# Gathering the rows of a further job when those of the one before it are turned, and one condition per expert on GpSimd

## The reference, cut to what matters

```python
def hier_moe(h, w_rg, b_rg, w_re, b_re, w_gate, w_up, w_down):
    n, t_len, d = h.shape
    x = h.reshape(-1, d)
    ...                      # top-1 of 4 groups, then top-2 of its 8 experts: 2 experts of 32 per token
    hg = jnp.einsum('md,edf->mef', x, w_gate)
    hu = jnp.einsum('md,edf->mef', x, w_up)
    act = jax.nn.silu(hg) * hu * combine[..., None].astype(x.dtype)
    y = jnp.einsum('mef,efd->md', act, w_down)
    return y.reshape(n, t_len, d)
```

## Time and profile before

| | |
|---|---|
| time, median of 3 | 1289.67 us |
| the profiled execution's own time | 1288.67 us |
| its span (first to last instruction) | 1286.9 us |
| TensorE matmul busy | 1086.6 us (84%) |
| VectorE / ScalarE / GpSimd busy | 381.4 / 228.4 / 187.9 us |
| mean granted TensorE clock | 0.926 |
| DMA, mean | 219 GB/s |

### The profile page before, as it was taken

The page is one execution under the profiler, slowest core; times in us unless marked ns, Lnnn a source line. Parts: engine busy times, 40 slices in busy tenths (PEclk is TensorE's granted clock), DMA queues, the critical chain, the costliest instruction groups (busy, mean ns, idle before and its releaser), DMA issues.

```text
span 1286.9 us, 19486 instructions
## 1 busy us (share of the span) xinstructions
PE 1086.6 (84%) x7107; PEld 682.5 (53%) x7108; DVE 381.4 (30%) x731; ACT 228.4 (18%) x413; POOL 187.9 (15%) x297
## 2 busy tenths in 40 slices
PE   5999998899679978888499999999599866797790
PEld 4887685675345534444177777644355433353440
DVE  2000013342342111111239899352432101021116
ACT  4000111344201111011230100261101000110112
POOL 0000100100022221211102111010032212122120
PEclk9999998999889998888799999999799888898895
DMA  9323124700547999999741100421749998399545
GB/s 364 152 92 144 36 78 73 289 2 21 212 167 307 406 409 408 408 405 409 307 167 67 66 2 2 152 114 40 303 169 409 404 354 340 113 396 361 226 164 226
DMA packets 71938, 281.90 MB, mean 219 GB/s; under 512 B 11614, under 2 KB 11678, under 8 KB 68576
## 3 DMA queue, kind: packets, MB, share of 16 engines
q1 hardware_dynamic: 55824, 251.66, 50.3%
q0 software_dynamic: 10800, 17.89, 4.0%
q10 hardware_dynamic: 5216, 11.10, 2.6%
HBM read 269.83 MB, written 29.65 MB: 233 GB/s over the span
## 4 chain that ended last, share of the span: by engine, by line
PE 49%; DMA 26%; DVE 12%; issue 5%; ACT 4%; POOLq 1%; POOL 1%; ACTq 0%; SPq 0%; DVEq 0%
DMA ring<-w_moe 14%; PE psum L1496 10%; DMA ar<-w_moe 7%; PE psum L1685 5%; PE psum L1604 5%; PE psum L1816 5%; DVE ar L1353 4%; PE psum L1490 3%; PE psum L1779 3%; DMA ar<-normed_rows,ixe 3%; PE psum L1740 3%; PE psum L1713 2%; PE psum L1547 2%; PE psum L1563 1%; DVE ar L1142 1%
## 5 line engine op out<-in xcount | busy, mean ns | idle before, releaser
L1685 PE MATMUL psum<-ring,ar 128*64 128x256 f32 x1408 | 179.2, 400 | 21.2 <-DMA ring<-w_moe 19.4
L1685 PEld LDWEIGHTS psum<-ring,ar 128*64 128x64 f32 x1408 | 102.4, 144 | 95.3 <-issue 32.0
L1496 PE MATMUL psum<-ar,ring 128*128 128x272 f32 x576 | 132.7, 393 | 0.0
L1816 PE MATMUL psum<-ar,ring 128*128 128x272 f32 x512 | 120.8, 398 | 3.0 <-DVE ar L1339 3.0
L1496 PEld LDWEIGHTS psum<-ar,ring 128*128 128x128 f32 x576 | 109.3, 190 | 22.9 <-issue 0.3
L1816 PEld LDWEIGHTS psum<-ar,ring 128*128 128x128 f32 x512 | 97.8, 192 | 28.0 <-issue 4.2
L1353 DVE SCALAR_TENSOR_TENSOR ar<-ar,sv 128x512 f32<-128x512 f32 x120 | 107.0, 893 | 5.8 <-ACT ar L900 1.9
L1685 PE MATMUL psum<-ar 128*64 128x256 f32 x640 | 85.6, 414 | 14.9 <-DMA ar<-w_moe 14.9
L1282 DVE COPY ar<-psum 128x128 f32<-128x128 f32 x64 | 18.7, 292 | 265.8 <-PE psum L1730 265.8
L1740 PE MATMUL psum<-ring,ar 128*64 128x512 f32 x352 | 84.1, 598 | 0.8 <-DVE ar L1282 0.4
L1604 PE MATMUL psum<-ring,ar 128*128 128x512 f32 x192 | 84.0, 594 | 0.0
(11 more groups left out here) (216 smaller groups left out, 1162.6 us busy)
## 6 DMA issues: line engine op xcount, KB each, us to landing
ring<-w_moe SPq DMA_DIRECT2D x44, 3072.0 KB, 16.8
ar<-w_moe SPq DMA_DIRECT2D x20, 3072.0 KB, 16.8
ring<-w_mix SPq DMA_DIRECT2D x4, 3072.0 KB, 20.9
ring<-w_pw SPq DMA_DIRECT2D x6, 2048.0 KB, 10.7
ring<-expert_outputs SPq DMA_DIRECT2D x8, 1024.0 KB, 7.9
ring<-kv_in SPq DMA_DIRECT2D x2, 2880.0 KB, 11.6
normed_rows<-ar ACTq DMA_DIRECT2D x8, 512.0 KB, 2.6
X<-x_in ACTq DMA_DIRECT2D x4, 512.0 KB, 9.6
```

Of the source, the lines that this page charges most:

```text
L1496: t = mm(psum[:, b + h, 0:HALF], w[:, k, P * c:P * c + P], hT[:, k, HALF * h:HALF * h + HALF], start=k == 0, stop=k == KD - 1)
L1685: t = mm(psum[64 * f:64 * f + 64, u % 2, 0:2 * P], xt[:, k, 64 * (u % 2):64 * (u % 2) + 64], w[:, k, f, :], start=k == 0, stop=k == KD - 1)
L1816: t = mm(psum[:, b + h, 0:HALF], w[:, k, o:o + P], hT2[:, k, HALF * h:HALF * h + HALF], start=k == 0, stop=k == KD - 1)
```

## The change

On GpSimd `further_first` and `further_rest` become one function, `further(it, u)`, which reads the count and, only if it isn't zero, the number in front. For each chunk c of the expert it first issues the gather of the rows of chunk c + 1 of the whole list, whatever expert that belongs to, once chunk c has been turned, and then sends out the result of c. The gather of the list's first chunk is issued ahead of the loop without a condition. After the list's last chunk one more gather is issued, whose indices are all out of bounds (`SKIP`), so that it moves no rows; the index table `tg` gets one more column for it, which VectorE fills with one more instruction, and GpSimd now waits for four tables and not three. The other engines' code for the further jobs is unchanged.

```diff
--- before.py
+++ after.py
@@ -158,7 +158,7 @@
         ixg = sb("ixg", [P, 3], I32)
         ixe = sb("ixe", [P, 1], I32)
         ixy = sb("ixy", [P, 4], I32)
-        tg = mb[:, 0:4 * MORE].bitcast(I32)
+        tg = mb[:, 0:4 * MORE + 2].bitcast(I32)
         jt = sb("jt", [1, 2 * EXPERTS], I32)
         psum = ctx.enter_context(nc.psum_tensor("psum", [P, 8, 512], F32))
 
@@ -556,7 +556,7 @@
                 nc.gpsimd.memset(xg[0], 0.0).then_inc(moe.rows_clear, 1)
                 pool.wait_ge(moe.jobs, n + 1)
                 nc.gpsimd.memset(xg[1], 0.0).then_inc(moe.rows_clear, 1)
-                pool.wait_ge(moe.tokens, 3 * n + 3)
+                pool.wait_ge(moe.tokens, 4 * n + 4)
                 nc.gpsimd.memset(xg[2], 0.0).then_inc(moe.rows_clear, 1)
                 pool.wait_ge(moe.xn_out, 16 * TILES * (n + 1))
 
@@ -573,15 +573,12 @@
                     pool.indirect_dma_start(xg[v], None, xn_dram, bass.IndirectOffsetOnAxis(ixg[:, v:v + 1], 0),
                                             bounds_check=TOK - 1, oob_is_err=False).then_inc(moe.rows_in[v], 16)
 
-                def counts(it, u):
-                    return (pool.value_load(jt[0:1, bass.ds(MSLOTS * it + (EXPERTS * what + u), 1)],
-                                            min_val=0, max_val=MORE) for what in range(2))
 
                 def chunk_rows(chunk):
 
                     pool.wait_ge(ex[n].turned, chunk + 1)
-                    o = nc.s_assert_within(chunk + MORE, MORE, 2 * MORE - 1,
-                                           skip_runtime_bounds_check_because="at most MORE chunks")
+                    o = nc.s_assert_within(chunk + MORE, MORE, 2 * MORE,
+                                           skip_runtime_bounds_check_because="at most MORE chunks and one empty")
                     nc.gpsimd.tensor_copy(ixe[0:JOB, 0:1], tg[0:JOB, bass.ds(o, 1)]).then_inc(ex[n].ix, 1)
                     pool.wait_ge(ex[n].ix, chunk + 1)
                     pool.sem_inc(moe.seen, 1)
@@ -599,21 +596,18 @@
                     pool.indirect_dma_start(ys_dram, bass.IndirectOffsetOnAxis(ixy[:, 3:4], 0), ye, None,
                                             bounds_check=4 * TOK - 1, oob_is_err=False).then_inc(ex[n].out, 16)
 
-                def further_first(it, u):
-
-                    chunks, before = counts(it, u)
+                def further(it, u):
+
+                    def count(what):
+                        return pool.value_load(jt[0:1, bass.ds(MSLOTS * it + (EXPERTS * what + u), 1)],
+                                               min_val=0, max_val=MORE)
+
+                    chunks = count(0)
                     with pool.If(chunks > 0):
-                        chunk_rows(before)
-
-                def further_rest(it, u):
-
-                    chunks, before = counts(it, u)
-                    with pool.If(chunks > 0):
-                        with pool.If(chunks > 1):
-                            with pool.Fori(1, chunks) as c:
-                                chunk_rows(before + c)
-                                chunk_out(before + c - 1)
-                        chunk_out(before + chunks - 1)
+                        before = count(1)
+                        with pool.Fori(0, chunks) as c:
+                            chunk_rows(before + c + 1)
+                            chunk_out(before + c)
 
                 def outputs(it, u):
 
@@ -625,13 +619,11 @@
                     pool.indirect_dma_start(ys_dram, bass.IndirectOffsetOnAxis(ixy[:, b:b + 1], 0), yj[b], None,
                                             bounds_check=4 * TOK - 1, oob_is_err=False).then_inc(moe.y_out[b], 16)
 
-                def body(it, gathers, jobs=MSLOTS, last=False):
+                def body(it, gathers, jobs=MSLOTS):
                     for u in range(jobs):
                         if u % 2 == 0 and gathers:
                             rows_of(3 * it + (u // 2 + 4), u + 8)
-                        further_rest(it, u)
-                        if not (last and u == jobs - 1):
-                            further_first(it, u + 1)
+                        further(it, u)
                         outputs(it, u)
 
 
@@ -639,12 +631,16 @@
                     rows_of(v, 2 * v, True)
                 nc.gpsimd.memset(xe, 0.0).then_inc(pool_link, 1)
                 pool.wait_ge(pool_link, 3 + 2 * n)
-                further_first(0, 0)
+                nc.gpsimd.tensor_copy(ixe[0:JOB, 0:1], tg[0:JOB, MORE:MORE + 1]).then_inc(ex[n].ix, 1)
+                pool.wait_ge(ex[n].turned, 1)
+                pool.wait_ge(ex[n].ix, 1)
+                pool.indirect_dma_start(xe, None, xn_dram, bass.IndirectOffsetOnAxis(ixe[0:JOB, 0:1], 0),
+                                        bounds_check=TOK - 1, oob_is_err=False).then_inc(ex[n].rows, 16)
                 rows_of(3, 6)
                 with pool.Fori(0, 4) as it:
                     body(it, True)
                 body(4, False)
-                body(5, False, EXPERTS % MSLOTS, True)
+                body(5, False, EXPERTS % MSLOTS)
 
             experts(0)
 
@@ -1253,6 +1249,8 @@
                                             ALU.arith_shift_right).then_inc(moe.tokens, 1)
                 nc.vector.tensor_scalar(tg[0:JOB, MORE:2 * MORE], tb[0:JOB, EXPERTS:JOBS], 2, None,
                                         ALU.arith_shift_right).then_inc(moe.tokens, 1)
+                nc.vector.tensor_scalar(tg[0:JOB, 2 * MORE:2 * MORE + 1], psum[0:JOB, 7, 0:1], 0.0, float(SKIP),
+                                        ALU.mult, ALU.add).then_inc(moe.tokens, 1)
 
                 def keep_rows(pair, first=False):
```

## The result

The changed kernel takes 1253.99 us (median of 4 runs, 1252.19 to 1255.05) against 1289.76 us before: 35.8 us less, a ratio of 0.9723 with the 95% interval 0.9706 to 0.9739. The forecast was 1246.7 us, 43.0 less. The profiled execution has a span of 1252.5 us, 34.4 less than before. Two single executions further down lie far outside their rows of the table, one of 2246 us (last row) and one of 1474 us (reordered, again); they are counted in the medians and left out of the ratios.

The account below looks back on a forecast made before the run. The first expert stage was taken as bound by weights, the second as held up by further jobs' gathers. 35.6 + 10.0 - 1.0 - 1.0 - 0.2 - 0.4 = 43.0 us gained, giving 1246.7 us; range 1242 to 1258.

Parts of the forecast that it names:

- signs of being wrong: Second stage of 274 us or more, chunk windows above 10 us without a wait, or waits ahead of 15 and 23.
- The waits that go: TensorE's five waits for gathered rows ahead of second-stage chunks all vanish: 35.6 us gained.
- The clock: Five chunks slowed by reduced TensorE clock after waits would take 8.81 us each at full clock: 10.0 us gained.
- the clock stays down: Rival: the chunks' own 0.4 to 0.9 us pauses keep TensorE's clock low; 34.0 us gained, 1255.7 us; chance 0.08.
- What is late next: Three new delays: expert 11's second chunk 1.0 us, the weights 1.0 us, GpSimd's loop 0.2 us.
- Second chunk of 11: Its gather, issued after the first chunk's turning, would land late and make TensorE wait: 1.0 us lost.
- Weights late in the stage: The second stage's weight stream may fall behind TensorE near expert 31: 1.0 us lost, bounds 0 and 18.
- GpSimd's loop: GpSimd's 10.5 us of standing still would make expert 15's gather late: 0.2 us lost.
- The added work: One more VectorE instruction in each layer's setup delays clearing of `xg[2]`: 0.4 us lost in two layers.
- The removed work: 91 GpSimd table reads go in the second stage, 26 us of its sequencer's time; counted as no gain.
- The slower rival: GpSimd pauses with each looped expert would decide the pace; 1300 us at 5.55 us per pause; chance 0.02.

Follow-up runs that it names:

- last row: Kernel before, gathers in their old places, second table read only where an expert has chunks, plus 40 never-executed instructions per expert on GpSimd: 1302.44 us, ratio 1.0089.
- reordered, again: Second measurement of the changed kernel with chunks moved ahead of pair turning (TensorE), product (VectorE) and pair gather (GpSimd): 1243.81 us, ratio 0.9626.
- the pauses filled: Changed kernel with useless matmuls in TensorE's pauses inside and ahead of chunks: 1253.28 us, ratio 0.9712.
- the reordered kernel: Changed kernel with chunks moved ahead of the next pair's turning on TensorE, the product on VectorE and the pair's gather on GpSimd: 1244.46 us, ratio 0.9642.
- the changed kernel's second: Changed kernel measured again, unaltered: 1255.72 us, ratio 0.9724.
- the long body in the new order: Changed kernel plus 40 semaphore instructions per expert on GpSimd under a condition never met: 1269.32 us, ratio 0.9839.
- in the old order the short body: Kernel before, no gather moved, second table read only where an expert has chunks (two reads per expert, not four): 1275.46 us, ratio 0.9885.
- the reads restored: Changed kernel with four table reads per expert on GpSimd again, three of them unused: 1257.53 us, ratio 0.9729.
- one with fillers: Changed kernel with chunks moved ahead on TensorE, VectorE and GpSimd, plus one useless matmul at each of two places within a chunk: 1245.95 us, ratio 0.9651.

## Why the forecast came out as it did

It was right in the mechanism that carries it: the five waits go, the first layer doesn't move, and the range holds the time. Of the 43.0 us, 34.4 are in the profiled execution. One of its own signs of being wrong came too: four of the chunks' windows are above 10 us with no gather to wait for. Step by step:

**The waits that go, 35.6.** Measured 35.6. The chunks of 15 and 23, whose gather goes out at the neighbour's turning, found their rows in time, as worked out.

**The clock, 10.0: the term that went wrong.** The six windows sum to 64.1 us; less the 3.5 us of longer pauses in them they are 60.6, so 2.2 us came, not 10.0. The argument was that the second chunk of expert 11 had the same pauses and ran at 1.00. That a chunk with such pauses runs at full clock was right: this second chunk did so in all seven profiles, reordered ones aside, in which nothing was filled and it began without a wait, and with the pauses filled, or cut to 0.88 us, no block of 24 is slow. But the other five chunks did not get its pauses. They got VectorE's, of 1.70 us ahead of the chunk or 1.93 to 2.24 us ahead of gate and up, and of the ten blocks with such a pause in the two profiles of the changed kernel eight are slow, not the same ones in both. With those pauses gone the term came: the reordered kernel's windows over a chunk are 8.91 us, so 53.5 for six, 9.4 less than before. The rival "the clock stays down" had chance 0.08 and 34.0 us, and is nearest to what was seen; but its condition was wrong, since pauses of 0.4 to 0.9 us leave the clock up. The Trainium skill (TensorE: Matmul & The Clock Gate, section "A second HAM failure mode: psum-queue depth-cycling") says that short idle times between groups of matmuls, if they come often enough, can throttle the array. The runs agree where the pauses are 1.7 to 2.2 us, and show nothing of it where they are 0.88 us at most.

**What is late next: VectorE, not in the list.** The forecast named the second chunk of 11, the weights and GpSimd's loop. It didn't ask what else TensorE's chunk line needs once the rows are there. The old waits of 4.96 to 11.39 us covered VectorE's emptying of the bank and its table reads behind the product; uncovered they cost 3.4 and 3.5 us, 6.9 in all, and through the clock the 7.7 us of slow blocks besides. This is the one omission behind both terms. The list of waits of before could not show them, since it names the latest releaser alone; the order of VectorE's code (`keep_rows` and the product ahead of `further`) did. The reordered kernel confirms both sizes: its second stage is 14.1 us shorter.

**The three losses that were named.** Second chunk of 11: 1.0 forecast, none measured, not even in the reordered kernel where 8.91 us lie between the turnings: its gather goes out at 1030.6 and lands 6.0 us later, 0.5 us ahead of the turning at 1037.14. Weights late in the stage: 1.0 forecast, none; the one wait, of 2.98 us, is at expert 11, where 3.89 us stood before. GpSimd's loop: 0.2 forecast, none, its pauses gone.

**The added work, 0.4.** The clearing of `xg[2]` starts at 941.75 in place of 941.69: 0.06 us in the second layer.

**Not in the sum: the weights early in the stage.** Expert 12's gate and up end at 1030.33 in place of 1033.45, 3.1 us earlier, since the weights of expert 11 are there 2.2 us earlier and the matmuls behind that wait are less slow. From the stage's start to expert 11's gate and up it was 71.6 us; in eight of nine profiles with the short body it is 69.3 to 69.7, in the ninth, the changed kernel's second, 72.4. With the long body in the new order it is 71.4. So it goes with the short body mostly, and its cause wasn't tried.

The sum that fits: 35.6 - 3.4 (ahead of chunks) - 1.3 (chunk windows, 64.1 against 62.8) + 3.1 = 34.0, of 34.4.

**Where it was lucky.** VectorE's pauses and the missing clock took 14.7 us from the forecast. That the time still lies in the range owes something to 3.1 us of weights that weren't in the sum and to some 2.5 us of named losses and added work that didn't come. Without them the gain would have been near 28.8 us and the time near 1260, above the range's 1258.

**The removed work.** "I count nothing" holds for the reads. It missed the length of the body that goes with them, though the pauses and their place were seen: in the old order the short body by itself took away two of the five waits, most of the 15 us. In the sum it doesn't add to the waits, since the moved gathers remove the same ones: with the long body in the new order none of the five is there.

**The slower rival.** Its pauses are real, but they come at the jump back and shortly behind it, not with each expert. The Trainium skill (Runtime: NRT & Kernel Launch, section "Instruction fetch mechanics") says that a taken branch outside a small window of blocks waits for a fetch. The long bodies agree in kind, with pauses of 3.7 to 4.8 us in the second layer. That a long body would cost its time in the *first* layer, through the weights, stood in no rival.

## What to carry to other kernels

When a wait goes, list everything else that the waiting instruction needs, with the time at which each would have been ready; the profile names the last one only, and the others surface at their full size. A recovered clock was worth counting here only once no pause near 2 us was left around the block: look for those first. Reordering took them away together with their own time; filling only kept the clock up. And in a loop on GpSimd the length of the body can be a cost of its own, even where the added code never runs.

## What the runs showed of the hardware

- Length of GpSimd's loop body: 25 to 30 instruction fetches and no pause over 2.1 us with the short one, 44 and six pauses of 4.25 to 5.55 us before (all in the second layer), 64 and 81, with pauses of 3.7 to 5.2 us, with 240 never-executed instructions per turn.
- With the long bodies the stream of weights in the first layer is slower by 9 and 16 us, with 0.3 to 0.4 MB more of instructions fetched in the whole run. TensorE waits for weights there, and the busy DMA engines move 389 and 376 GB/s in place of 408. That the fetches hold up the weights on the same DMA engines would explain it, but this was only argued; no run took the fetches away and kept the body, and it stays open.
- TensorE's granted clock after pauses of 1.7 to 2.2 us: reduced in 8 blocks of 10 in the changed kernel and in 2 of 5 with the reads restored, and different for the same chunk in two executions of one kernel. After pauses of 0.88 us at most it was full in 18 chunks of 18 (two profiles of the reordered kernel and one with fillers).
